# RWKV-7 recurrence of a two-layer encoder on one core: the products of a block in two bank pairs by kind, the state product in a bank of its own, N as block-diagonal 128x128 weights, roots grouped, Y last, scans in the tail

## The reference, cut to what matters

```python
def step(state, inp):
    r_t, w_t, k_t, v_t, kk_t, a_t = inp
    sa = jnp.einsum('bhvk,bhk->bhv', state, -kk_t)
    state = (state * w_t[:, :, None, :] + sa[..., None] * (kk_t * a_t)[:, :, None, :]
             + v_t[..., None] * k_t[:, :, None, :])
    y = jnp.einsum('bhvk,bhk->bhv', state, r_t)
    return state, y
```

## Time and profile before

| what | value |
|---|---|
| 3 timed runs | 3403.66, 3412.59, 3413.34 us (median 3412.59) |
| the profiled execution | 3416.12 us, of which the profile's span is 3414.1 us |
| TensorE clock, mean granted share over the span | 0.944 |
| recurrence: loads at 1894, first transposes at 1924.8, last store issued at 2517.7 | 624 us |
| one pair in the middle (first transposes of pair 3 to those of pair 4) | 2131.6 to 2202.7, 71.1 us |

### The profile page before, as it was taken

The page is one execution under the profiler, slowest core; times in us unless marked ns, Lnnn a source line. Parts: engine busy times, 40 slices in busy tenths (PEclk is TensorE's granted clock), DMA queues, the critical chain, the costliest instruction groups (busy, mean ns, idle before and its releaser), DMA issues.

```text
span 3414.1 us, 64714 instructions
## 1 busy us (share of the span) xinstructions
PE 3010.4 (88%) x26866; PEld 2392.9 (70%) x26866; DVE 1668.4 (49%) x2253; ACT 1066.9 (31%) x1559; POOL 1449.6 (42%) x1459
## 2 busy tenths in 40 slices
PE   5988587899999999999999578888758999999997
PEld 5734365677778877877788477777747877877886
DVE  4488895465454545465121244444333543444345
ACT  2255465413111221125421454455411311211122
POOL 1201000144566566665365334443333566556553
PEclk6899899999999999999999799999979999999998
DMA  6300000341232223222532211111021111111111
GB/s 204 115 1 13 1 2 1 118 154 52 78 92 74 66 75 92 75 65 74 181 99 86 76 47 65 60 53 48 22 94 43 31 53 52 40 41 54 51 40 70
DMA packets 230046, 226.97 MB, mean 66 GB/s; under 512 B 16430, under 2 KB 198273, under 8 KB 229825
## 3 DMA queue, kind: packets, MB, share of 16 engines
q1 hardware_dynamic: 216368, 177.27, 16.9%
q10 hardware_dynamic: 13457, 46.45, 3.8%
HBM read 185.67 MB, written 37.75 MB: 65 GB/s over the span
## 4 chain that ended last, share of the span: by engine, by line
PE 43%; issue 19%; POOL 18%; DVE 9%; DMA 5%; ACT 3%; POOLq 1%; ACTq 0%; SPq 0%; DVEq 0%; PEldq 0%; PEld 0%
POOL w_hi L149 9%; POOL w_lo L151 8%; PE ps L139 7%; PE ps L141 7%; PE ps L140 7%; DMA w_raw<-in_f_w_up_dram 2%; PE ps L2412 2%; DVE d_junk L1368 2%; PE ps L2424 2%; PE ps L1142 2%; DMA w_raw<-in_f_w_down_dram 2%; PE ps L1165 1%; PE ps L1154 1%; PE ps L2368 1%; PE ps L2445 1%
## 5 line engine op out<-in xcount | busy, mean ns | idle before, releaser
L149 POOL TENSOR_TENSOR w_hi<-w_raw,ones 128x128 fp32r<-128x128 f32 (+1 forms) x568 | 468.2, 824 | 1136.3 <-PE ps L141 1010.5
L139 PE MATMUL ps<-hn_hi,w_hi 128*128 128x512 f32 x1408 | 553.6, 393 | 26.4 <-POOL w_lo L151 18.2
L151 POOL TENSOR_TENSOR w_lo<-w_raw,w_hi 128x128 fp32r<-128x128 f32 (+1 forms) x568 | 555.4, 978 | 44.5
L749 DVE SCALAR_TENSOR_TENSOR uc<-u,pc,uc 128x1024 f32<-128x1024 f32 x176 | 277.5, 1577 | 596.7 <-ACT uc L733 584.5
L140 PE MATMUL ps<-hn_lo,w_hi 128*128 128x512 f32 x1408 | 550.4, 391 | 0.0
L141 PE MATMUL ps<-hn_hi,w_lo 128*128 128x512 f32 x1408 | 550.3, 391 | 0.0
L732 ACT ACTIVATE u<-ps 128x1024 f32<-128x1024 f32 x88 | 90.5, 1028 | 939.3 <-PE ps L141 934.6
L139 PEld LDWEIGHTS ps<-hn_hi,w_hi 128*128 128x128 f32 x1408 | 266.0, 189 | 90.3 <-issue 18.6
L141 PEld LDWEIGHTS ps<-hn_hi,w_lo 128*128 128x128 f32 x1408 | 265.8, 189 | 55.6
L140 PEld LDWEIGHTS ps<-hn_lo,w_hi 128*128 128x128 f32 x1408 | 266.2, 189 | 54.6
L139 PE MATMUL ps<-g_hi,w_hi 128*128 128x512 f32 x704 | 279.9, 398 | 10.8 <-POOL w_lo L151 9.9
(11 more groups left out here) (346 smaller groups left out, 5566.9 us busy)
## 6 DMA issues: line engine op xcount, KB each, us to landing
w_raw<-in_f_w_up_dram SPq DMA_DIRECT2D x88, 512.0 KB, 3.9
f_ada_w<-in_ada_w_dram SPq DMA_DIRECT2D x48, 512.0 KB, 3.9
rwkv_scratch<-rp_stage ACTq DMA_DIRECT2D x48, 512.0 KB, 3.0
w_raw<-in_f_w_down_dram SPq DMA_DIRECT2D x176, 128.0 KB, 2.2
rc_raw<-rwkv_scratch SPq DMA_DIRECT2D x32, 512.0 KB, 3.6
d_r<-in_ada_w_dram ACTq DMA_DIRECT2D x24, 512.0 KB, 5.4
ada_w<-in_ada_w_dram SPq DMA_DIRECT2D x16, 512.0 KB, 8.5
xin<-in_x_dram SPq DMA_DIRECT2D x8, 512.0 KB, 7.3
```

The costliest lines, as they stand in the source:

```text
L139: pe.matmul(out, w_hi, x_hi, start=first, stop=False)
L149: pool.tensor_tensor(hi, raw, one, ALU.mult).then_inc(k.w_hi_done, 1)
L151: pool.tensor_tensor(k.w_lo[s][:, tiles, :], raw, hi.bitcast(F32), ALU.subtract).then_inc(k.w_split if n else k.w_half, 1)
L749: dve.scalar_tensor_tensor(out=c[wi][:, :], in0=u[wi][:, tap:tap + S], scalar=k.pc[:, bass.ds(i * (2 * FF_TILES) + col, 1)], in1=c[wi][:, ...
```

## The change

It rewrites the recurrence's order and its use of PSUM. In the part on the edits, "removed" are the products with the removed key b, "keys" those with k.

- The six planes are split: four (N, its transpose, b with a and r) in the bank pair 2/3, two (k with a and r) in the bank pair 0/1. Each has its own masks on DVE, so masking a block is three instructions of 128x256 and not one of 128x512 and one of 128x256.
- The chain no longer adds to S. DVE scales all of S at once in the tail (`given_dve`, into `sx`), PE writes each step's product to a bank of its own (`step_out`, bank 7), and DVE combines them (`state_dve`). `q_t` and `mt` now lie in the weight buffers `w_raw`.
- N times U uses a block-diagonal copy of N (`nbd`), one matmul of 128x128 weights for each block and head in place of two of 64x64. ACT fills it with two small copies for each block (`spread_act`).
- Sums of squares and their maxima move from the levels into the product phase, in quarters; the bonus products are spread over blocks 0 to 3.
- ACT: the logarithms stand together after levels 1 to 3, the exponentials after level 3; the negation moves to POOL; the program has 31 ACT_TABLE_LOADs and had 44.
- Tail: Q and M stand ahead of Y. The scans of pair p+2 stand at the end of pair p. Before pair 0 and after pair 7 DVE does part of POOL's work.

```diff
-    UPD = STEPS - 1
-    G_BR, G_KA, G_KR, G_N = range(4)
+    UPD = STEPS - 2
+    G_BR, G_N, G_KA, G_KR = range(4)
+    QUARTER = S // 4
+    BONUS = BLK // 2
+    SUMS = 4
...
+    nbd = sb("nbd", [P, BLK, 2, P])
...
+    sx = sb("sx", [P, BLK, 2, C64])
+    q_t, mt = (k.w_raw[i][:, :, :].rearrange("p a (b t) -> p (a b t)", t=C64).rearrange("p (c x t) -> p c x t", c=2, t=C64)
+               for i in range(2))
...
+    def sum_out(q, i):
+        return bank(0)[:, QUARTER:2 * QUARTER] if q else bank(i)[:, 0:QUARTER]
...
+    step_out = bank(7)[:, 0:C64]
...
+    def removed_pe(pe, p, x):
+        u, g = p % 2, planes(REMOVED, 4)
         if x:
-            for n in ("g_sb", "x_sb"):
-                pe.wait_ge(sem[n], BLK * p + x)
+            pe.wait_ge(sem["g2_sb"], 2 * (BLK * p + x))
+            if x == BONUS:
+                pe.wait_ge(sem["bon"], 2 * p + 2)
         else:
             pe.wait_ge(sem["ar1"], p + 1)
+            pe.wait_ge(sem["ar0"], p + 1)
+            pe.wait_ge(sem["bt"], p + 1)
             if p:
                 pe.wait_ge(sem["q_sb"], 4 * p)
+            else:
+                pe.wait_ge(sem["max"], SUMS)
+        if x < BONUS:
+            bon_pe(pe, p, x)
         for c in range(2):
             for h in range(2):
-                pe.matmul(gn[hs(c), h, 4 * C64:5 * C64], ar[u][hs(h), x, 0, hs(c)], b_t[hs(h), toks[c]],
+                pe.matmul(g[hs(c), h, 0:P].rearrange("p (i t) -> p i t", i=2), b_t[hs(h), toks(x, c)],
+                          ar[u][hs(h), x, :, hs(c)], start=True, stop=True)
...
+        last.then_inc(sem["g2_ps"], 1)
...
+    def key_pe(pe, p, x):
+        u, g, more = p % 2, planes(KEYS, 2), p + 1 < PAIRS
+        if x:
+            pe.wait_ge(sem["g3_sb"], BLK * p + x)
+            if more and x > BLK - SUMS:
+                pe.wait_ge(sem["max"], SUMS * (p + 1) + x - (BLK - SUMS))
+        else:
+            pe.wait_ge(sem["kt"], p + 1)
+            if p:
+                pe.wait_ge(sem["sx"], 2 * p)
+        if more and x >= BLK - SUMS:
+            sums_pe(pe, p + 1, x - (BLK - SUMS))
+        for c in range(2):
+            for h in range(2):
+                last = pe.matmul(g[hs(c), h, :].rearrange("p (i t) -> p i t", i=2), k_t[hs(h), toks(x, c)],
+                                 ar[u][hs(h), x, :, hs(c)], start=True, stop=True)
+        last.then_inc(sem["g3_ps"], 1)
...
     def chain_pe(pe, p, e):
         x, c = e // 2, e % 2
         if e == 0:
             return
-        pe.wait_ge(sem["s_sb"], UPD * p + e)
         if e == 1:
+            pe.wait_ge(sem["sx"], 2 * p + 2)
+            pe.wait_ge(sem["q_ps"], 3 * p + 3)
             pe.wait_ge(sem["q_sb"], 4 * p + 4)
-        now = state[e % 2]
-        if e < UPD:
+        else:
+            pe.wait_ge(sem["s_sb"], UPD * p + e - 1)
+        now = state[e % 2] if e > 1 else sx[:, 0, 0, :]
+        if e <= UPD:
             for h in range(2):
-                last = pe.matmul(bank(c)[hs(h), at(x)], mt[hs(h), c, x, :], now[hs(h), :],
-                                 start=False, stop=True, skip_group_check=True)
+                last = pe.matmul(step_out[hs(h), :], mt[hs(h), c, x, :], now[hs(h), :], start=True, stop=True)
             last.then_inc(sem["s_ps"], 1)
...
-                for c in range(2):
-                    last = pe.matmul(bank(4 + h)[hs(1 - c), at(x)], gm[hs(c), x, h, G_N, :], ul[hs(c), 0, h, x, :],
-                                     start=True, stop=True)
+                last = pe.matmul(bank(4 + h)[:, at(x)], nbd[:, x, h, :], ul[:, 0, h, x, :], start=True, stop=True)
...
+            h, x0 = i // 2, 4 * (i % 2)
+            if i % 2 == 0:
+                pe.wait_ge(sem["u_sb"][h], 5 * p + 5)
...
+    def spread_act(act, p, x):
+        act.wait_ge(sem["g2_sb"], 2 * (BLK * p + x) + 1)
+        for c in range(2):
+            act.activation(nbd[hs(c), x, :, hs(1 - c)], gm[hs(c), x, :, G_N, :], ACT.Copy).then_inc(sem["n_sb"], 1)
...
+    def given_dve(dve, p):
+        dve.wait_ge(sem["s0_ps"], p + 1)
+        dve.wait_ge(sem["pend"], p + 1)
+        for c in range(2):
+            factor = p_end[p % 2][:, :].rearrange("p (x c) -> p x c", c=2)[:, :, c:c + 1].to_broadcast([P, BLK, C64])
+            dve.tensor_tensor(sx[:, :, c, :], bank(c).rearrange("p (x t) -> p x t", t=C64), factor, ALU.mult
+                              ).then_inc(sem["sx"], 1)
+
     def state_dve(dve, p, e):
-        x, c = e // 2, e % 2
-        dve.wait_ge(sem["s_ps"], UPD * p + e + 1)
-        if e == 0:
-            dve.wait_ge(sem["pend"], p + 1)
-        dve.tensor_scalar(state[(e + 1) % 2][:, :], bank(c)[:, at(x)], p_end[p % 2][:, e:e + 1], None, ALU.mult
-                          ).then_inc(sem["s_sb"], 1)
-
-    def masked_dve(dve, p, x):
-        dve.wait_ge(sem["g_ps"], BLK * p + x + 1)
-        gn = two(1)
-        four = upper[:, :, :].rearrange("p i c -> p (i c)").unsqueeze(1).to_broadcast([P, 2, 4 * C64])
-        dve.tensor_tensor(gm[:, x, :, :, :].rearrange("p h i c -> p h (i c)"), gn[:, :, C64:5 * C64], four, ALU.mult
-                          ).then_inc(sem["g_sb"], 1)
+        if e == 0 or e > UPD:
+            return
+        dve.wait_ge(sem["s_ps"], UPD * p + e)
+        dve.scalar_tensor_tensor(out=state[(e + 1) % 2][:, :], in0=step_out, scalar=p_end[p % 2][:, e:e + 1],
+                                 in1=sx[:, e // 2, e % 2, :], op0=ALU.mult, op1=ALU.add).then_inc(sem["s_sb"], 1)
+
+    def removed_dve(dve, p, x):
+        dve.wait_ge(sem["g2_ps"], BLK * p + x + 1)
+        g = planes(REMOVED, 4)
+        both = upper[:, 0:2, :].rearrange("p i c -> p (i c)").unsqueeze(1).to_broadcast([P, 2, P])
+        dve.tensor_tensor(gm[:, x, :, G_BR:G_N + 1, :].rearrange("p h i c -> p h (i c)"), g[:, :, C64:3 * C64], both,
+                          ALU.mult).then_inc(sem["g2_sb"], 1)
         if x == 0:
             dve.wait_ge(sem["id_sb"], 3 * p + 3)
-        src = gn[:, :, 0:6 * C64].rearrange("p h (i c) -> p i h c", c=C64)[:, 0:6:5, :, :]
+        src = g[:, :, :].rearrange("p h (i c) -> p i h c", c=C64)[:, 0:4:3, :, :]
         dve.copy_predicated(ul[:, :, :, x, :], first[:, 0:2, :].unsqueeze(2).to_broadcast([P, 2, 2, C64]), src
-                            ).then_inc(sem["x_sb"], 1)
+                            ).then_inc(sem["g2_sb"], 1)
+
+    def key_dve(dve, p, x):
+        dve.wait_ge(sem["g3_ps"], BLK * p + x + 1)
+        both = upper[:, 2:4, :].rearrange("p i c -> p (i c)").unsqueeze(1).to_broadcast([P, 2, P])
+        dve.tensor_tensor(gm[:, x, :, G_KA:G_KR + 1, :].rearrange("p h i c -> p h (i c)"), planes(KEYS, 2), both, ALU.mult
+                          ).then_inc(sem["g3_sb"], 1)
...
-        sums_pe(pe, 0)
+        for i in range(SUMS):
+            sums_pe(pe, 0, i)
         for p in range(PAIRS):
+            transposes_pe(pe, p, 0)
+            removed_pe(pe, p, 0)
             for x in range(BLK):
-                transposes_pe(pe, p, x)
                 if p:
                     chain_pe(pe, p - 1, 2 * x)
-                products_pe(pe, p, x)
+                key_pe(pe, p, x)
                 if p:
                     chain_pe(pe, p - 1, 2 * x + 1)
-                if x == 2:
-                    bon_pe(pe, p)
+                if x + 1 < BLK:
+                    removed_pe(pe, p, x + 1)
+                    transposes_pe(pe, p, x + 1)
             up_pe(pe, p)
             for lv in LV:
                 levels_pe(pe, p, lv)
-                if lv == 1 and p + 1 < PAIRS:
-                    sums_pe(pe, p + 1)
             tail_pe(pe, p)
...
+                if x:
+                    spread_act(act, p, x - 1)
...
+            spread_act(act, p, BLK - 1)
             if p:
                 y_act(act, p - 1)
...
             for lv in LV:
                 for s in range(2):
                     levels_act(act, p, lv, s)
-                    if more and (lv, s) in ((2, 1), (3, 0)):
+                    if more and (lv, s) in ((1, 1), (2, 0)):
                         ln_act(act, q, 1 - s)
+                    if p and (lv, s) == (3, 0):
+                        log_act(act, p - 1)
+                    if p and (lv, s) == (3, 1):
+                        root_act(act, p - 1)
                     if more and (lv, s) in ((3, 1), (4, 0)):
                         rs_act(act, q, 1 - s)
-                    if p and (lv, s) == (4, 0):
-                        root_act(act, p - 1)
             tail_act(act, p)
         y_act(act, PAIRS - 1)
+        log_act(act, PAIRS - 1)
         root_act(act, PAIRS - 1)
...
             for x in range(BLK):
+                removed_dve(dve, p, x)
+                if x == BONUS - 1:
+                    bon_dve(dve, p)
                 if p:
                     state_dve(dve, p - 1, 2 * x)
-                masked_dve(dve, p, x)
-                if p and 2 * x + 1 < UPD:
+                key_dve(dve, p, x)
+                if more and x == BONUS:
+                    rkw_dve(dve, q)
+                if p == 0 and x in (1, 2):
```

(43 more changed lines are left out.)

255 lines of the change are left out of this document (132 added, 123 removed).

## The result

The changed kernel takes 3406.3 us (median of 20 runs, 3401.6 to 3415.4) against 3413.6 for the kernel before on the same chips (20 runs): ratio 0.998, 95% interval 0.9973 to 0.9987. It is faster by 0.2%, where 3358 was forecast; the time lies outside the range, and within the 10 us that the prediction itself called no change.

A forecast was written before the change was run, and what follows sets the result against it. No engine is full; loops between engines set the pace. Six pairs -32, pair 0 -3, pair 7 -8, ends -8 and -4: -55 on 3416.1 gives 3361; the median 3.5 below gives 3358 us, range 3318 to 3392.

The forecast's parts named there:

- Scans and pieces: Product phase: moving scans to the tail saves 1.6 us a pair; bonus and sums pieces add 0.45 x 3 + 0.2 x 4 = 2.2.
- The 1.3 for the first round: Product phase: first round's 5.07 us exceeds the steady one by 2.6; half of that excess, 1.3, was counted as gone.
- Half hides behind DVE: Product phase: sums of squares come as four pieces of 0.45 us, half of which hides behind DVE's work.
- Steps 1 and 2: Product phase: shorter rounds -3.8 us, scans moved -1.6, pieces +2.2, first round -1.3; together -4.5 a pair.
- now all count: Levels: issue waits of 1.5 us a pair add fully to five levels' 28.7, giving 30.2 against 29.8.
- Steps 3 and 4: Levels +0.4 us a pair, with N's wider loads; W/U products starting on one head's U, -0.7.
- Step 5: Tail: Y behind Q and M covers DVE's q_t and mt, -0.5 us a pair; the 2.19 issue wait stays.
- the fallback that the prediction named: Before pair 0: if POOL and DVE disturb one another, 1.8 us per instruction and -5 in place of -8.
- The clock stays up and the issue waits shrink: Rival: 1.3 us of clock and 2 of issue waits a pair more, -23, 3335 us; chance 0.20.
- Slow rounds: Rival: product rounds stay near 2.3 us, through ACT or DVE work not fitting; +20, 3380 us; chance 0.15.
- No effect: Rival: a new wait, b or w late, takes what the rounds give; 3413 us; chance 0.04.
- the three signs by which the forecast was to be known as wrong: N's records at 0.06 or 0.17 us, product rounds above 2.2 us, or PE waiting for POOL's b.

The follow-up runs named there:

- the last two kernels: Changed kernel with 64x64 N, sums in levels, transfers out of the tail: 3355.0 us; same, but gain, store and g starting in the next product phase's first rounds: 3352.1 us.

## Why the prediction was wrong, point by point

A pair of 1 to 6 was to gain 5.3 us and gained 0.65. By steps, on their mean:

1. *Round of the product phase:* 1.99 forecast, 2.12 measured. The mechanism was right (mask, predicated copy and state step of 0.34, 0.33 to 0.47 and 0.37); PE and no longer DVE closes the round.
2. *Scans and pieces:* the scans cost nothing in the tail, as forecast. The pieces are the mis-sized term: eight pieces cost 0.4 to 0.84, about 5 in all, where 2.2 stood. The round with the scans gave some of it back: it lasted 5.18 on the mean of pairs 1 to 6, and 4.06 only in pairs 3 and 6. The 1.3 for the first round came from pair 3 alone: its 5.07 held an issue wait of 1.5 and half clock, and not only waits for DVE, and in pairs 1, 2, 4, 5 and 6 this round lasted 2.47 to 3.40. It is 2.13 now. "Half hides behind DVE" failed, since PE is the bound of the rounds it made, and a change between 128-row and 64-row products costs beside the records (some 0.25, worked out below). Steps 1 and 2 gave -2.4 for -4.5.
3. *Levels:* right. N's records at 0.111 to 0.116, levels 28.9, +1.5 a level. That issue waits "now all count" was wrong in our favour: fewer instructions, hardly any waits. Steps 3 and 4 gave -1.1 for -0.3; the up products took 0.3 more. What no step saw is that before's levels were held by the fetch (3.6 us of issue waits a pair, of which the prediction counted 1.5), so that undoing the wide N brings not the 7.5 of its records but 2.6.
4. *Tail:* the step that failed. "-0.5; the issue wait of 2.19 inside M stays" became +2.5: issue waits of 3.4 a pair where they were 1.5, and half clock behind the two longest (3.4 and 3.5). The prediction counted the transfers of moved steps only for whether their data comes in time, not for what they do to PE's fetch. Moving three of the five, and the gain, gave 12 us by the ratios and 18 by the medians. Step 5's own idea was worth far more than its 0.5: Y last keeps PE busy up to the product phase, which is worth 36 us, most of it by the clock. It is no full cure, as two phases of the kernel with 64x64 N and one of that with more loads show. In the kernel before, half clock cost less: pair 2 had 10.2 us more of it in its product phase than pair 1, and the phase was 3.1 us longer. That DVE's loop, and not PE's clock, set most of its rounds would explain this; it was not tried.
5. *Pair 0* was to gain 3 and lost 7.4. Its product phase took 25.3 us for 21.4: the pieces run at half clock (rounds of 3.68) and one wait that the profile calls issue is 1.1 (the one of 15 that does not end behind a packet); it has no chain whose loop could have shrunk. The levels pay +1.2, the tail +1.9. This is read from the trace and was not tried by itself, though without the sums in it (the last two kernels) it took 23.1.
6. *Ends:* behind pair 7 as forecast (five instructions of 1.22 to 1.23 on DVE). Ahead of pair 0 the fallback that the prediction named came, -5.6: DVE's and POOL's instructions stretch each other,

```profile
1907.21 1.22 DVE L2243 TENSOR_TENSOR rc_km<-rc_km,rc_raw 128x1024 f32<-128x1024 f32 x1
...
1914.80 3.37 DVE L2276 TENSOR_TENSOR rc_raw<-rc_kk,rc_raw 128x1024 f32<-128x1024 f32 x1
```

   the second beside POOL's kt (3.33 for 2.35 alone). The Trainium skill (SBUF — State Buffer, section SBUF: two separate sides) says that a DVE operation with two SBUF inputs and one of GpSimd exclude each other for the whole instruction. The trace agrees in kind: 3.37 is about the sum of one POOL instruction, 2.35, and DVE's own 1.22.

Of the rivals, none was this. "The clock stays up and the issue waits shrink" (0.20) had its conditions met, the clock at 1.00 in the product phases and no issue waits in the levels, and yet not its 3335: part of the waits came back in the tail, and the clock is part of the product phase's 2.4, not a gain on top. "Slow rounds" had the right side of the product phase, which makes up a third of the miss. "No effect" (0.04) has the nearest number for a reason that did not occur, b or w late. Of the three signs by which the forecast was to be known as wrong, one came in part, rounds above 2.2 (the five of seven with a piece); none looked at the tail.

What stays open: that what the profile calls issue is here the instruction fetch is inferred, from waits that end at a fixed distance behind instruction packets, that come and go with the number of instructions and that grow with data transfers; no record names it, or the engine that a packet is for. Waits of about 0.8 us at the up and W/U products of the kernel before mostly do not fit it. Why the clock fell in one product phase and not in the next is open too. The 0.3 us by which the up products grew was not looked into.

## What to carry to other kernels

Before a dense stretch of small matrix products is trusted to its record times, count its instructions against the packets of the instruction queue, and look at which data transfers the change puts beside it: their place is set by engines that are off the critical path. A level bound by fetch makes an edit with fewer but slower records look free, and hides what undoing it would bring. Where PE waits just ahead of a phase that PE itself bounds, fill or move the wait: waits of 1.3 us were followed here by a phase 7.6 us longer.
